# Prompt attention in turns of long and short query tiles, with two output banks and wider-set stages

## The reference, cut to what matters

```python
kc, vc = compress(rows_c, pe_k, pe_v, phi_k, phi_v)     # 31 compressed keys
o_c, p_c = cmp_attend(q, pos, kc, vc)
idx = select_blocks(p_c, pos, S // SEL_BLK)
o_s = sel_attend_blocked(q, pos, idx, rows_s, SEL_QBLK)
o_w = window_attend_prompt(q, rows_w)
y = nsa_combine(gates, o_c, o_s, o_w, w_out)
```

## Time and profile before

| | |
|---|---|
| median of 3 runs | 1717.38 us (1716.52 to 1719.98) |
| the profiled execution | 1711.65 us, of which the span is 1710.0 us |
| PE busy in the span | 1595.6 us (93%) |
| DVE, ACT, POOL busy | 785.8, 687.2, 219.1 us |
| the attention stage, first scores to last product with the values | 950.93 to 1139.84 us |

### The profile page before, as it was taken

One profiled execution on the slowest core, in us unless ns is written; L12 is line 12 of the kernel. 1 busy time (PEld: TensorE's weight loads), 2 busy tenths in 40 slices (PEclk: granted clock), 3 DMA queues, 4 the chain that ended last, 5 costly groups with the idle time before them and its releaser, 6 DMA issues.

```text
span 1710.0 us, 31077 instructions
## 1 busy us (share of the span) xinstructions
PE 1595.6 (93%) x12951; PEld 1453.0 (85%) x12951; DVE 785.8 (46%) x1274; ACT 687.2 (40%) x1312; POOL 219.1 (13%) x582
## 2 busy tenths in 40 slices
PE   5999989899999999978999899988969999999996
PEld 3999978699999999968999555555959999999995
DVE  4555453455531555344112565653165553255523
ACT  3122134355532555222322465654335552255422
POOL 3000001200000000001013244431100000000000
PEclk8999999999999999987999899999979999999998
DMA  6132217223233232324334100013302323323231
GB/s 213 51 100 75 99 56 176 59 59 89 71 101 91 83 90 70 96 74 160 109 111 88 50 2 2 1 35 115 86 25 74 85 72 95 101 83 87 63 90 52
DMA packets 185559, 138.46 MB, mean 81 GB/s; under 512 B 11376, under 2 KB 177504, under 8 KB 185392
## 3 DMA queue, kind: packets, MB, share of 16 engines
q1 hardware_dynamic: 175536, 106.31, 21.8%
q0 software_dynamic: 9920, 30.74, 5.9%
HBM read 128.21 MB, written 13.01 MB: 83 GB/s over the span
## 4 chain that ended last, share of the span: by engine, by line
PE 66%; DVE 6%; ACT 3%; issue 2%; DMA 2%; POOLq 1%; POOL 1%; DVEq 0%; ACTq 0%
PE gemm L853 40%; PE gemm L585 10%; PE gemm L601 6%; PE misc L560 4%; DMA raw<-in_o_w_in 2%; PE gemm L987 2%; PE misc L1018 1%; DVE y L1550 1%; ACT pr L1162 1%; DVE pr L1833 1%; DVE y L1540 1%; DVE xT L1554 1%; POOLq L493 1%; DVE hL L1527 1%; PE misc L621 1%
## 5 line engine op out<-in xcount | busy, mean ns | idle before, releaser
L1516 DVE TENSOR_TENSOR wL<-raw,wH 128x2048 fp32r<-128x2048 f32 (+2 forms) x107 | 222.1, 2076 | 240.1 <-ACT wH L1162 240.1
L853 PE MATMUL gemm<-hH,wH 128*128 128x272 f32 x1280 | 268.4, 291 | 0.0
L853 PE MATMUL gemm<-hH,wL 128*128 128x272 f32 x1280 | 264.8, 288 | 0.0
L853 PE MATMUL gemm<-hL,wH 128*128 128x272 f32 x1280 | 264.0, 288 | 0.0
L1162 ACT ACTIVATE wH<-raw 128x2048 fp32r<-128x2048 f32 (+2 forms) x107 | 185.2, 1731 | 61.1 <-PE gemm L585 32.7
L853 PEld LDWEIGHTS gemm<-hH,wH 128*128 128x128 f32 x1280 | 200.5, 188 | 5.9 <-issue 4.9
L853 PEld LDWEIGHTS gemm<-hL,wH 128*128 128x128 f32 x1280 | 201.1, 188 | 0.0
L853 PEld LDWEIGHTS gemm<-hH,wL 128*128 128x128 f32 x1280 | 199.9, 189 | 0.0
L601 PE MATMUL gemm<-wH,hH 128*128 128x256 f32 x560 | 163.9, 293 | 12.8 <-DVE hL L1527 9.2
L1753 DVE SCALAR_TENSOR_TENSOR conv<-up,rows_t,conv 128x560 f32<-128x560 f32 x88 | 70.5, 801 | 214.3 <-ACT conv L1162 214.3
L601 PE MATMUL gemm<-wL,hH 128*128 128x256 f32 x560 | 161.5, 288 | 0.0
(11 more groups left out here) (331 smaller groups left out, 2659.2 us busy)
## 6 DMA issues: line engine op xcount, KB each, us to landing
raw<-in_f_w_in SPq DMA_DIRECT2D x88, 512.0 KB, 4.9
raw<-in_f_w_out SPq DMA_DIRECT2D x32, 704.0 KB, 4.6
raw<-in_e_w_in SPq DMA_DIRECT2D x12, 1024.0 KB, 5.1
raw<-in_o_w_in SPq DMA_DIRECT2D x10, 1024.0 KB, 5.2
raw<-in_e_w_out SPq DMA_DIRECT2D x4, 1024.0 KB, 5.6
pages<-in_cache_cmp POOLq DMA_DIRECT2D x16, 256.0 KB, 3.5
raw<-in_o_w_out SPq DMA_DIRECT2D x16, 256.0 KB, 5.5
rows<-in_cache_sel POOLq DMA_DIRECT2D x12, 256.0 KB, 2.9
```

Of the source, the lines that this page charges most:

```text
L853: ins = pe.matmul(gemm[odd][:, n, 0:TH], w, x[:, k, n * TH:(n + 1) * TH], start=(k == 0 and part == 0), stop=(k == nk - 1 and part == 2))
L1516: order(dve.tensor_tensor(unit_view(wL, u), unit_view(raw, u), unit_view(wH, u).bitcast(F32), ALU.subtract), lo_ready)
```

## The change

It changes the order of the units, the banks, the queue orders and the engine that copies a unit.

- `LAG` goes from 3 to 4, and `turn_probs` is issued ahead of `scores` in a turn.
- Units of the long tiles (3 and 2) and of the short tiles (0 and 1) alternate, after four units of tile 0 alone. The long stream is tiles 3, 2 of j = 0, then 3, 2 of j = 1 and sums into bank 2; the short stream is tiles 0, 1, 0, 1 and sums into bank 3. At the end four long units (384 keys) are left alone.
- On ACT the copy comes first, and the exponentials are those of unit n-1. On DVE the copy comes first, then the mask of unit n, then the normalising of unit n-2.
- Copies go to ACT for two units, then to DVE for two.
- `turn_in` uses bank 2 in turns 1 to 6, and the sample tokens' key transposes behind the stage use bank 3, after a wait on `o_lo`.

```diff
-        N_UNITS, LAG = 72, 3
+        N_UNITS, LAG = 72, 4
+
+        LONG, SHORT = [(0, 3), (0, 2), (1, 3), (1, 2)], [(0, 0), (0, 1), (1, 0), (1, 1)]
+        streams = [[(bank, pos, w) for pos in range(4) for w in range(9)] for bank in range(2)]
+        AHEAD = 4
+        SEQUENCE = streams[1][:AHEAD]
+        for x, y_ in itertools.zip_longest(streams[0], streams[1][AHEAD:]):
+            SEQUENCE += [x] if y_ is None else [x, y_]
 
         def attention_unit(n):
-            grp, w = n // 9, n % 9
-            return grp // 4, grp % 4, w, (w - 1) // 2, (w - 1) % 2
+
+            bank, pos, w = SEQUENCE[n]
+            j, qt = (LONG, SHORT)[bank][pos]
+            return j, qt, w, (w - 1) // 2, (w - 1) % 2
...
         def on_vector(n):
 
-            return n % 2 == 1
+            return (n // 2) % 2 == 1
...
+        def turn_bank(n):
+
+            return 2 + n % 2 if n < 6 else 2
...
             for n in range(N_UNITS + LAG + 1):
+                if LAG <= n < N_UNITS + LAG:
+                    turn_probs(n - LAG)
                 if n < N_UNITS:
-                    if n % 36 == 0:
+                    if n in (0, SECOND_HALF):
                         for sem_ in qk_ev:
-                            pe.wait_ge(sem_, 3 + 3 * (n // 36))
+                            pe.wait_ge(sem_, 6 if n else 3)
                     scores(n)
                 if 1 <= n < 7:
                     turn_in(5 + n)
-                if LAG <= n < N_UNITS + LAG:
-                    turn_probs(n - LAG)
                 if n > LAG:
                     mix_values(n - LAG - 1)
...
             for n in range(N_UNITS + LAG + 2):
-                if n < N_UNITS:
-                    exps(n)
+                if LAG <= n < N_UNITS + LAG:
+                    take_probs(n - LAG)
+                if 1 <= n <= N_UNITS:
+                    exps(n - 1)
                 if 1 <= n < 7 and n % 2:
                     take_in(5 + n)
-                if LAG <= n < N_UNITS + LAG:
-                    take_probs(n - LAG)
-                if n >= LAG + 10 and (n - LAG - 10) % 9 == 0:
-                    heads_hi((n - LAG - 10) // 9)
+                if n - LAG - 2 in GROUP_ENDS:
+                    heads_hi(n - LAG - 2)
...
             for n in range(N_UNITS + LAG + 2):
+                if LAG <= n < N_UNITS + LAG:
+                    take_probs(n - LAG)
                 if n < N_UNITS:
                     mask(n)
                 if 1 <= n < 7 and n % 2 == 0:
                     take_in(5 + n)
-                if 1 <= n < N_UNITS + 1:
-                    normalise(n - 1)
-                if LAG <= n < N_UNITS + LAG:
-                    take_probs(n - LAG)
-                if n >= LAG + 10 and (n - LAG - 10) % 9 == 0:
-                    heads_lo((n - LAG - 10) // 9)
+                if 2 <= n < N_UNITS + 2:
+                    normalise(n - 2)
+                if n - LAG - 2 in GROUP_ENDS:
+                    heads_lo(n - LAG - 2)
```

More of the change, by code:

```diff
@@ L432, in sample_heads, with out_bank, cmps_done, recips_done @@
             return dst, src[:, :, j, g2, 0:R, :].rearrange("p b r n -> p r b n")
-        N_UNITS, LAG = 72, 3
-        def attention_unit(n):
-            grp, w = n // 9, n % 9
-            return grp // 4, grp % 4, w, (w - 1) // 2, (w - 1) % 2
-        def masks_done(n):
[L443 to L449, removed]
-        def on_vector(n):
-            return n % 2 == 1
+        N_UNITS, LAG = 72, 4
[5 more added lines that the diff above has]
+            SEQUENCE += [x] if y_ is None else [x, y_]
+        def attention_unit(n):
+            bank, pos, w = SEQUENCE[n]
+            j, qt = (LONG, SHORT)[bank][pos]
+            return j, qt, w, (w - 1) // 2, (w - 1) % 2
+        def out_bank(n):
+            return 2 + SEQUENCE[n][0]
+        def cmps_done(n):
+            return sum(unit[2] == 0 for unit in SEQUENCE[:n + 1])
+        def recips_done(n):
+            return n + 1 - cmps_done(n)
+        def exps_done(n):
+            return 2 * recips_done(n)
+        def masks_done(n):
+            return exps_done(n) + cmps_done(n)
+        def on_vector(n):
+            return (n // 2) % 2 == 1
+        def copies_done(n):
+            return sum(on_vector(z) == on_vector(n) for z in range(n + 1))
+        GROUP_ENDS = [n for n in range(N_UNITS) if SEQUENCE[n][2] == 8]
+        def banks_taken(n):
+            bank, pos, _ = SEQUENCE[n]
+            return 1 + GROUP_ENDS.index(SEQUENCE.index((bank, pos - 1, 8))) if pos else 0
+        def cmp_factors_used(n):
+            earlier = [z for z in range(n) if SEQUENCE[z][2] == 0]
+            return masks_done(earlier[-1]) if earlier else 0
+        SECOND_HALF = min(n for n in range(N_UNITS) if attention_unit(n)[0] == 1)
+        def turn_bank(n):
+            return 2 + n % 2 if n < 6 else 2
         TURNS = [(0, z) for z in range(R + 2)] + [(1, R), (1, R + 1)] + [(1, z) for z in range(R)]
@@ L1005, in mix_values @@
                 j, qt, w, r, br = attention_unit(n)
-                grp = n // 9
-                pe.wait_ge(p_ev[n % 2], n // 2 + 1)
+                pe.wait_ge(p_ev[on_vector(n)], copies_done(n))
                 if w == 0:
-                    if grp >= 2:
-                        pe.wait_ge(o_lo, grp - 1)
+                    if banks_taken(n):
+                        pe.wait_ge(o_lo, banks_taken(n))
+                    elif out_bank(n) == 2:
+                        for sem_ in qk_ev:
+                            pe.wait_ge(sem_, 6)
                     for g2 in range(2):
-                        ins = pe.matmul(misc[64 * g2:64 * g2 + 64, 2 + grp % 2, :], vcP[:, j, g2 * HD:(g2 + 1) * HD], pT[0:NCP, n % 2, g2, :],
+                        ins = pe.matmul(misc[64 * g2:64 * g2 + 64, out_bank(n), :], vcP[:, j, g2 * HD:(g2 + 1) * HD], pT[0:NCP, n % 2, g2, :],
                                         start=True, stop=False, skip_group_check=True)
@@ L1025, in turn_in @@
                 j, z = TURNS[n]
-                bank = 2 + n % 2 if n < 6 else 3
+                bank = turn_bank(n)
                 if n >= 6:
@@ L1086, in turn_outputs @@
                 turn(gemm[1][:, b // 4, (b % 4) * P:(b % 4 + 1) * P], oS[:, b % 2, :], os_turned if b == DB - 1 else None)
+            pe.wait_ge(o_lo, 7)
             for z in range(4):
-                turn(misc[:, 2, z * NS:(z + 1) * NS], kvN[0:NS, 0, (2 * (z // 2) + 2) * 256 + (z % 2) * P:(2 * (z // 2) + 2) * 256 + (z % 2 + 1) * P],
+                turn(misc[:, 3, z * NS:(z + 1) * NS], kvN[0:NS, 0, (2 * (z // 2) + 2) * 256 + (z % 2) * P:(2 * (z // 2) + 2) * 256 + (z % 2 + 1) * P],
                      kn_turned if z == 3 else None, k=NS)
@@ L1426, in take_probs, with heads_hi @@
                 activate(pT[0:k, n % 2, :, 0:keys], misc[0:k, 0:2, 0:keys], ACT.Copy, p_ev[0])
[L1428 to L1431, removed]
+            def heads_hi(n):
+                j, qt, _, _, _ = attention_unit(n)
+                act.wait_ge(v_done, n + 1)
+                activate(hH[:, 4 * j:4 * j + 4, NS + qt * P:NS + (qt + 1) * P], misc[:, out_bank(n), :].rearrange("p (c q) -> p c q", c=4), ACT.Copy, o_hi)
             def take_in(n):
@@ L1861, in take_probs, with heads_lo @@
                 order(dve.tensor_copy(pT[0:k, n % 2, :, 0:keys], misc[0:k, 0:2, 0:keys]), p_ev[1])
-            def heads_lo(grp):
-                j, qt, _, _, _ = attention_unit(9 * grp)
-                dve.wait_ge(o_hi, grp + 1)
+            def heads_lo(n):
+                j, qt, _, _, _ = attention_unit(n)
+                dve.wait_ge(o_hi, GROUP_ENDS.index(n) + 1)
                 cols = slice(NS + qt * P, NS + (qt + 1) * P)
-                order(dve.tensor_tensor(hL[:, 4 * j:4 * j + 4, cols], misc[:, 2 + grp % 2, :].rearrange("p (c q) -> p c q", c=4),
+                order(dve.tensor_tensor(hL[:, 4 * j:4 * j + 4, cols], misc[:, out_bank(n), :].rearrange("p (c q) -> p c q", c=4),
                                         hH[:, 4 * j:4 * j + 4, cols].bitcast(F32), ALU.subtract), o_lo)
```

26 lines of the change are left out of this document (13 added, 13 removed).

## The result

The changed kernel takes 1722.54 us (median of 20 runs, 1717.46 to 1729.07) against 1717.55 us for the kernel before (20 runs): a ratio of 1.0031 [1.0019, 1.0043]. I had forecast 1713.2, 4.2 us less; it takes 5.0 us more.

What follows compares the result with a forecast made beforehand. PE was taken as the bound, busy 93%, its waits the gain. The stage would end at 971.0 + 146.9 + 17.7 = 1135.6 instead of 1139.8, 4.2 us less: 1717.4 - 4.2 = 1713.2 us, range 1702 to 1724.

Steps and rivals of the forecast that it cites:

- The copies go: PE's waits ahead of the probabilities' transposes for copies out of PSUM, 10.6 us, were to go.
- The loop: Reciprocal n behind mask n+2 on DVE: PE waits 1.0 us for POOL, 512-key pairs take 5.25 us, 384-key pairs 4.36.
- From unit 4 to the end of the stage: Thirty pairs from unit 4's transposes, 146.9 us, then the last pair and four 384-key units, 17.7 us.
- the added wait on `o_lo`: Wait ahead of the sample keys' transposes behind the stage: costed at nothing; without cover, 1.3 us.
- The fill: Eight turns at the stage's start, ahead of the first long unit's transposes, which were to start at 971.0.
- the sign that I had named: The prediction called itself wrong if the fill at the stage's start lasted past 973.
- The clock behind the fill: PE's clock in the stage: no fall taken, and the one fall of before was to go, worth 2.7 us.
- The rival by which it falls again and again: Clock falls repeatedly in 512-key pairs, 2.7 us each; slower from three falls, 1724.0 us with four; chance 0.20.
- The rule that I cited: PE idling briefly between matmul groups can swing the clock; the regular 1.0 us wait would then harm beyond its length.

Runs made afterwards that it cites:

- after_again: The changed kernel run once more with no edit: 1721.83 us, 1.0033 against the kernel before.
- next_heads_warm: Changed kernel with normalise(n-1) on DVE, `heads_hi`/`heads_lo` earlier in their turn, five extra matmuls at the stage's start: 1696.47 us; repeated as _2 on another chip, 1700.33 us.
- norm_first: Changed kernel with normalise(n-2) moved ahead of mask(n) on DVE: 1706.88 us, 0.9956 against the kernel before.
- after: The changed kernel as first measured and profiled: 1722.54 us, 1.0031 against the kernel before.
- norm_third: Changed kernel with normalise(n-3) in place of normalise(n-2), behind mask(n) on DVE: 1877.95 us, 1.0934 against the kernel before.
- units_in_order: Changed kernel's queue orders with units in the order of before and banks by turns of groups: 1706.48 us, 0.9947 against the kernel before.

## Why the prediction was wrong, point by point

**The copies go**: right. 10.6 us became 0.6.

**The loop**: right in its mechanism and in its size. A 512-key pair lasts 5.27 us for 5.25. The 384-key pairs follow each other at 4.35 and 4.36 (transposes at 1030.50, 1034.85 and 1039.21) for 4.36. The sum of the waits for POOL, 11.5 us, is under the 14 to 18 that I wrote; I had counted 1.0 us for more pairs than have it. Beside a 256-key unit PE has more work in the gap, and the wait is 0.39 (1020.72) for 0.93. The time of the pairs doesn't rest on that count.

**From unit 4 to the end of the stage**: 146.9 + 17.7 = 164.6 forecast, 168.0 in `after_again` at full clock. The tail is the 17.7 (1129.95 to the stage's end at 1147.5). Of the 3.4 left, 2.4 are the wait for `heads_lo`. **This is a step that I didn't take**: I weighed the added wait on `o_lo` behind the stage, and not that with one bank for each stream the next nine units add into the bank that DVE is still to read. About 1.0 us stays unassigned.

**The fill**: 20.1 forecast, 23.4 measured, twice. **This is the step that failed**: the term was 3.3 us too small, and the sign that I had named (the fill lasts past 973) came true. I carried over the clock of before, back at its upper level by about 962, that is 11 us after the first scores, though the recorded text doesn't say so; in the changed kernel it came back 21 us after them. Below stand three rows of before, then four steps in `after_again`, then two of the same steps in `next_heads_warm`:

```profile
955.00:960.00 5.00, 3.20 (x15) 2.47 (x16) 2.59 (x14) 3.52 (x16) 1.84 (x4) 0.50 0.00 0
960.00:965.00 5.00, 5.00 (x30) 3.06 (x29) 2.05 (x12) 2.40 (x7) 1.39 (x4) 0.81 0.00 0
...
959.55 1.91 PE L560 MATMUL misc<-ident_sb,pr 128*31 128x128 f32 x8
...
959.51 1.92 PE L600 MATMUL misc<-ident_sb,pr 128*31 128x128 f32 x8 [0.45 <-POOL pr L2145]
...
968.97 2.08 PE L1027 MATMUL gemm<-ksT,qT 64*128 64x512 f32 x4
970.98 1.11 PE L600 MATMUL misc<-ident_sb,qN 128*128 128x128 f32 x4
...
974.57 1.06 PE L600 MATMUL misc<-ident_sb,pr 128*31 128x128 f32 x8 [0.86 <-POOL pr L2145]
...
957.26 1.04 PE L600 MATMUL misc<-ident_sb,pr 128*31 128x128 f32 x8
...
964.35 0.66 PE L600 MATMUL misc<-ident_sb,qN 128*128 128x128 f32 x4
```

Up to the transposes of unit 0 (959.51 in `after_again`) nothing is lost: 8.3 us after the first scores, for 8.6 in before. From there to the end of unit 6's scores (971.0) PE goes from step to step without idle time, at a clock of 0.50 throughout, and takes 11.5 us; from before's 959.55 to the forecast's 967.4 there are 7.9, and `next_heads_warm` does the same steps in 7.1 at 1.00 (957.26 to 964.35). The chain behind (mask, copy, normalising, POOL) is as forecast, 3.5 for 3.6. So the loss lies in PE's own steps at the lower clock. Why the clock stays down for longer is open: `norm_first` doesn't wait ahead of the transposes of unit 0 and has 17 us of half clock in its fill all the same.

**The clock behind the fill**: I took no fall, and one that was to go as worth 2.7. The first profile has two falls and `after_again` none. Between those profiles the part behind the fill differs by 170.65 - 168.03 = 2.6, so a fall costs 1.3 by this estimate from two executions. That is half of my price, but these falls are also only about half as long as the 7 us that I had priced. The rival by which it falls again and again is out: it decides from three falls on, and there are two and none. That the measured 1722.5 is near its 1724.0 is chance.

Put together for `after_again`: -4.2 + 3.3 (fill) + 2.4 (`heads_lo`) + 1.0 = +2.5, as measured (191.4 - 188.9). With the two falls of the first profile, 5.1. The medians differ by 5.0 and 5.6; the 2.5 to 3.1 us between these and the stage of `after_again` stay open. (Behind the stage `after` and `after_again` take 574.2 us each, where before takes 570.2; but `norm_first` takes 569.0 there, so this is not shown to come from the change.) The price of the loop was right, and still the sign was wrong: the gain of 4.2 was a small difference of large terms (10.6 of copies gone, most of it given back to POOL), and a fill that was sized 3.3 us too short, with a wait of 2.4 that I had at nothing, turned it.

The rule that I cited, of the Trainium skill (TensorE: Matmul & The Clock Gate, "A second HAM failure mode: psum-queue depth-cycling"), is that short idle gaps between groups of matmuls can make the clock swing. `after_again` disagrees: with 0.9 us of waiting in each pair of 512- and 128-key units it was granted 1.00 from 974.57 to the stage's end. The first profile, with the same waits, had its two falls; `norm_third`, which waits 94.5 us in all ahead of its transposes, agrees with a mean of 0.68.

## What to carry to other kernels

When a step moves in a hand-written queue, find for its result the last instruction that must now precede it on its own engine, and count the consumer's work that lies between what releases that instruction and the consumer: 2.2 us of room for 3.2 us of path gave, before anything ran, 1.0 us of wait and a pair of 5.25 us beside a 128-key unit, and 0.93 and 5.27 came. Do the same for every buffer that the new order uses again sooner, output banks and the steps at the end of a turn included. And undo the parts of a change one by one: here the new queue orders with the units in their old order gained 9.7 us, the new place of one reciprocal cost 15 us beside the alternation, and the alternation neither gave nor took anything that the runs can tell once the reciprocal was moved.

## What I had not expected of the hardware

The clock stayed at its lower level for 17 us in the fill of `after_again` and for some 33 in the stage of `units_in_order` while PE was busy for most of it (15.5 of 17.2 us in the first). Two stretches of the latter:

```profile
970.00:980.00 10.00, 10.00 (x54) 5.91 (x52) 3.30 (x18) 3.51 (x16) 2.63 (x6) 0.50 0.11 30
980.00:990.00 10.00, 10.00 (x48) 5.07 (x46) 5.31 (x23) 2.88 (x11) 3.44 (x7) 0.50 0.54 179
```

PE is busy 20.0 of 20 us at 0.50; a busy PE in the records is no sign that the clock comes back soon. And the same program is granted different clocks in different executions: with the same code, two short falls behind the fill (`after`) and none (`after_again`), and half clock in the fill of 6.8 us (`next_heads_warm_2`) and of none (`next_heads_warm`, on another chip). The clock of a single profile is a weak base for a price.
